# Work items of 32 rows instead of 64 in the routed-expert stage of a decoder step

## The reference, cut to what matters

```python
def swiglu(x, wg, wu, wd):
    return (jax.nn.silu(x @ wg) * (x @ wu)) @ wd
# routed: out[row] += weight * swiglu(h2[row], w_gate[e], w_up[e], w_down[e])   for the row's 8 experts e
# w_gate, w_up: 1024 x 256, w_down: 256 x 1024, all float32, 3.15 MB for each expert
```

## Time and profile before

| | us |
|---|---|
| median of 3 runs | 1567.07 |
| lowest, highest | 1562.95, 1567.58 |
| the profiled execution | 1568.95 |
| its span, first to last instruction | 1567.2 |
| PE busy in the span | 1495.0 (95%) |
| DVE, ACT, POOL busy | 649.3, 357.8, 211.9 |
| mean granted clock of TensorE | 0.976 |
| moved by DMA | 437.26 MB, mean 279 GB/s |

### The profile page before, as it was taken

How to read it: one execution, slowest core, us unless ns; L and a number is a source line. 1 busy time by engine, 2 the same in 40 slices (tenths; PEclk the granted TensorE clock), 3 DMA queues, 4 the chain that set the end, 5 groups by cost and what they waited for, 6 DMA issues and landing times.

```text
span 1567.2 us, 22305 instructions
## 1 busy us (share of the span) xinstructions
PE 1495.0 (95%) x8198; PEld 815.4 (52%) x8198; DVE 649.3 (41%) x1126; ACT 357.8 (23%) x674; POOL 211.9 (14%) x257
## 2 busy tenths in 40 slices
PE   4999999999999989999999989999999999999988
PEld 4444456777688768878545533333333333333333
DVE  4899992332231576437567811111111111111136
ACT  4111133422443324332124111111111111111120
POOL 2231101111000013100000011111111211111100
PEclk9999999999999899899999999999999999999998
DMA  9798645878422567638411699999999999989696
GB/s 341 263 324 293 248 139 194 283 278 287 145 81 81 181 210 261 228 108 302 137 54 54 242 364 419 420 419 421 370 384 407 371 421 420 416 297 414 261 368 253
DMA packets 124759, 437.26 MB, mean 279 GB/s; under 512 B 17702, under 2 KB 45722, under 8 KB 89854
## 3 DMA queue, kind: packets, MB, share of 16 engines
q1 hardware_dynamic: 95728, 323.73, 54.6%
q0 software_dynamic: 23616, 101.90, 17.5%
q10 hardware_dynamic: 5344, 10.65, 1.8%
HBM read 507.52 MB, written 45.61 MB: 353 GB/s over the span
## 4 chain that ended last, share of the span: by engine, by line
PE 83%; DMA 9%; DVE 3%; ACT 2%; issue 1%; SPq 1%; ACTq 0%; POOLq 0%; DVEq 0%
PE bank L2525 19%; PE bank L2139 14%; PE bank L2050 12%; PE bank L2550 9%; PE bank L2370 4%; DMA arena<-in_w_exp_up_dram 4%; PE bank L2358 4%; PE bank L2511 3%; PE bank L2172 2%; DMA shared_rows<-arena 1%; DMA arena<-expert_rows 1%; PE bank L2597 1%; PE bank L2396 1%; PE bank L2535 1%; PE bank L2157 1%; PE bank L2297 1%
## 5 line engine op out<-in xcount | busy, mean ns | idle before, releaser
L2525 PE MATMUL bank<-arena 128*64 128x512 f32 x1536 | 345.6, 601 | 7.5 <-DMA arena<-in_w_exp_up_dram 6.4
L2139 PE MATMUL bank<-arena 128*128 128x260 f32 x1024 | 239.8, 390 | 0.0
L2525 PEld LDWEIGHTS bank<-arena 128*64 128x64 f32 x1536 | 106.6, 136 | 210.4 <-issue 205.3
L2139 PEld LDWEIGHTS bank<-arena 128*128 128x128 f32 x1024 | 193.4, 193 | 34.5 <-ACT arena L998 2.7
L2050 PE MATMUL bank<-arena 128*128 128x512 f32 (+1 forms) x448 | 190.4, 581 | 0.0
L2550 PE MATMUL bank<-arena 128*64 128x512 f32 x768 | 175.3, 598 | 0.5 <-ACT arena L1232 0.5
L1903 DVE TENSOR_TENSOR arena<-arena,bank 128x256 f32<-128x256 f32 x48 | 20.3, 423 | 362.3 <-ACT arena L1208 362.3
L2050 PEld LDWEIGHTS bank<-arena 128*128 128x128 f32 x448 | 83.8, 190 | 98.2 <-issue 90.7
L2550 PEld LDWEIGHTS bank<-arena 128*64 128x64 f32 x768 | 50.7, 136 | 89.4 <-issue 83.1
L1208 ACT ACTIVATE arena<-bank 128x256 f32<-128x256 f32 x48 | 18.5, 385 | 335.0 <-PE bank L2525 321.8
L1919 DVE COPY arena<-bank 128x512 f32<-128x512 f32 x48 | 33.3, 693 | 137.1 <-PE bank L2550 137.1
(11 more groups left out here) (469 smaller groups left out, 1567.0 us busy)
## 6 DMA issues: line engine op xcount, KB each, us to landing
arena<-in_w_exp_gate_dram SPq DMA_DIRECT2D x96, 1024.0 KB
arena<-in_w_exp_up_dram SPq DMA_DIRECT2D x96, 1024.0 KB
arena<-in_w_exp_down_dram SPq DMA_DIRECT2D x96, 1024.0 KB
arena<-in_w_ada_dram SPq DMA_DIRECT2D x24, 1024.0 KB, 7.4
arena<-in_w_merge_gate_dram SPq DMA_DIRECT2D x16, 1024.0 KB, 6.5
arena<-expert_rows SPq DMA_DIRECT2D x16, 1024.0 KB, 10.8
arena<-in_w_in_dram SPq DMA_DIRECT2D x6, 2048.0 KB, 14.3
gate_logits<-arena ACTq DMA_DIRECT2D x32, 260.0 KB, 4.9
```

Source lines behind the costliest of these rows:

```text
L2139: last = mm(o[:, 0:HALF], gate_place(q)[:, c, ms], hT[:, c, row_half[u % 2]], start=(c == 0), stop=(c == KC - 1))
L2525: ins = mm(bank[gu_bank[q]][r, :].rearrange("p (g n) -> p g n", g=2), xT[q][:, c, r], wgu[2 * q + lane][:, :, c, :], start=(c == 0), stop= ...
```

## The change

Items have 32 rows. A block still gathers 128 rows, 64 of lane 2q and 64 of lane 2q + 1, but these are now two items of each lane, and they are worked on in two half steps h = 0 to 5 within a round of three blocks. A half step has one item of 32 rows of each of two lanes. The lane pair of half step h is h % 3, so each lane's weight places are used every third half step. `gate_up` of a half step has 32 products of 256 columns with 32 stationary rows, over four column groups (two lanes, two halves of the hidden width); `down` has 8 products of 512 columns, again over four groups (two lanes, two halves of the output width). `middle_transposed` is one transpose per half step. The weights of half step g are asked for after `gate_up` of half step g - 3, the down weights after `down` of g - 3. The down weights are read as runs of 4 KB instead of 8 KB. The scatter of a block becomes two scatters of 2 KB per row. The tables have 102 columns of half steps instead of 66 of blocks and 204 cells instead of 132, and a few small VectorE operations are added to build them. The diff, cut to its core:

```diff
-SUB = 64
+SUB = 32
 LANES = 6
-MAXP = 22
+MAXP = 17
...
+            w_expert = [A[name][0].rearrange("e (p c) n -> e p (c n)", p=P) for name in ("w_exp_gate", "w_exp_up")]
+            w_expert_down = A["w_exp_down"][0].rearrange("e (c p) n -> e p c n", p=P)
+
+            def cell_expert(cell):
+                return sp.value_load(expert_p[:, bass.ds(cell, 1)], min_val=0, max_val=MISS)
 
             def gate_up_lanes(cell, b, lanes=range(2)):
                 for lane in lanes:
-                    expert_load([wgu[2 * b + lane][:, m, :, :].rearrange("p c n -> p (c n)") for m in range(2)], (0, 1), cell + lane, f"wg{b}")
+                    e = cell_expert(cell + lane)
+                    for m in range(2):
+                        dst = wgu[2 * b + lane][:, m, :, :].rearrange("p c n -> p (c n)")
+                        sp.dma_start(dst.unsqueeze(1), w_expert[m][bass.ds(e % NE, 1)].rearrange("e p n -> p e n"), cond=e < NE).then_inc(sem[f"wg{b}"], 16)
 
             def down_lanes(cell, b, lanes=range(2)):
                 for lane in lanes:
-                    expert_load([None, None, wdn[2 * b + lane].rearrange("p c n -> p (c n)")], (2,), cell + lane, f"wd{b}")
-
-            def gate_up_load(p, q):
-
-                sp.wait_ge(sem["gu_done"], p * 3 + (q - 3))
+                    e = cell_expert(cell + lane)
+                    sp.dma_start(wdn[2 * b + lane].unsqueeze(1), w_expert_down[bass.ds(e % NE, 1)].rearrange("e p c n -> p e c n"), cond=e < NE).then_inc(sem[f"wd{b}"], 16)
+
+            def gate_up_load(p, h):
+
+                sp.wait_ge(sem["gu_done"], p * 6 + (h - 2))
                 sp.sem_inc(sem["x_col"], 1)
-                gate_up_lanes(p * 6 + (2 * q - 2), block_at(p, q, -1)[1])
-
-            def down_load(p, q):
-
-                sp.wait_ge(sem["dn_done"], p * 3 + (q - 4))
+                gate_up_lanes(p * 12 + 2 * h, h % 3)
+
+            def down_load(p, h):
+
+                sp.wait_ge(sem["dn_done"], p * 6 + (h - 2))
                 sp.sem_inc(sem["x_col"], 1)
-                down_lanes(p * 6 + (2 * q - 4), block_at(p, q, -2)[1])
+                down_lanes(p * 12 + 2 * h, h % 3)
...
-            gate_up_load(1, 1)
-            gate_up_load(1, 2)
-            down_load(1, 2)
-            with sp.Fori(2, last + 1) as p:
-                for q in range(3):
-                    gate_up_load(p, q)
-                    down_load(p, q)
-            gate_up_load(last + 1, 0)
-            down_load(last + 1, 0)
-            down_load(last + 1, 1)
+            gate_up_load(0, 3)
+            gate_up_load(0, 4)
+            down_load(0, 3)
+            gate_up_load(0, 5)
+            down_load(0, 4)
+            with sp.Fori(1, last + 1) as p:
+                for h in range(6):
+                    gate_up_load(p, h)
+                    down_load(*half_at(p, h, -1))
+            down_load(last, 5)
...
-            sp.wait_ge(sem["gu_done"], last * 3 + 1)
+            sp.wait_ge(sem["gu_done"], last * 6 + 4)
...
+            half_rows = yd.rearrange("r (m d) -> (r m) d", m=2)
+
+            def block_scatter(p, q, at):
+
+                pb, qb = block_at(p, q, -5)
+                for a, evicted in enumerate(("y_a", "y_v")):
+                    pool.wait_ge(sem[evicted], pb * 3 + (qb + 1))
+                    pool.sem_inc(sem["x_col"], 1)
+                    pool.indirect_dma_start(out=half_rows, out_offset=bass.IndirectOffsetOnAxis(ap=at[:, 1 + a:2 + a], axis=0), in_=ybuf[qb][:, a * 512:(a + 1) * 512],
+                                            in_offset=None, bounds_check=2 * TOK * TOPK - 1, oob_is_err=False).then_inc(sem[f"yst{qb}"], 16)
...
+            def gate_up(p, h):
+                g, q, a, b = p * 6 + h, h // 2, h % 2, h % 3
+                pe.wait_ge(sem[f"wg{b}"], p * 128 + 64 * (h // 3 + 1))
+                if a == 0:
+                    pe.wait_ge(sem["x_ca"], p * 3 + (q + 1))
+                    pe.wait_ge(sem["x_cv"], p * 3 + (q + 1))
+                if later(p) or h >= 3:
+
+                    pe.wait_ge(sem["m_h"], g - 2)
                 for c in range(KC):
                     for lane in range(2):
+                        tokens = xT[q][:, c, 64 * lane + SUB * a:64 * lane + SUB * a + SUB]
+                        for n in range(2):
+                            r = slice(64 * lane + SUB * n, 64 * lane + SUB * n + SUB)
+                            ins = mm(bank[gu_bank[b]][r, 0:2 * P].rearrange("p (g n) -> p g n", g=2), tokens, wgu[2 * b + lane][:, :, c, n * P:(n + 1) * P], start=(c == 0), stop=(c == KC - 1))
                 ins.then_inc(sem["gu_done"], 1)
+            def middle_transposed(p, h):
+                g = p * 6 + h
+                pe.wait_ge(sem["m_h"], g + 1)
+                if later(p) or h >= 2:
+
+                    pe.wait_ge(sem["m_hTc"], g - 1)
+                tr(bank[4][:, h % 2 * P:h % 2 * P + P], hmid[h % 3], ident).then_inc(sem["m_hT"], 1)
+
+            def down(p, h):
+                g, q, a, b = p * 6 + h, h // 2, h % 2, h % 3
+                pe.wait_ge(sem["m_hTc"], g + 1)
+                pe.wait_ge(sem[f"wd{b}"], p * 64 + 32 * (h // 3 + 1))
                 if later(p) or q:
+                    pe.wait_ge(sem["y_v" if a else "y_a"], p * 3 + q)
+                for n in range(2):
+                    for lane in range(2):
+                        for m in range(2):
+                            r = slice(64 * lane + SUB * m, 64 * lane + SUB * m + SUB)
+                            ins = mm(bank[5 + a][r, :], hmT[b][:, 64 * lane + SUB * n:64 * lane + SUB * n + SUB], wdn[2 * b + lane][:, n, m * 512:(m + 1) * 512], start=(n == 0), stop=(n == 1))
                 ins.then_inc(sem["dn_done"], 1)
+            def block(p, q, front=True):
+
+                gate_up(p, 2 * q)
+                down(*half_at(p, 2 * q, -1))
+                middle_transposed(p, 2 * q)
+                gate_up(p, 2 * q + 1)
                 if front:
                     rows_transposed(*block_at(p, q, 1))
+                down(p, 2 * q)
+                middle_transposed(p, 2 * q + 1)
...
+            def block(p, q, front=True):
+                gate(p, 2 * q)
+                middle(p, 2 * q)
+                gate(p, 2 * q + 1)
                 if front:
                     rows_half(*block_at(p, q, 1))
-                if back:
-                    result_half(*block_at(p, q, -1))
-                middle(p, q)
+                result_half(p, q)
+                middle(p, 2 * q + 1)
...
+            def block(p, q, front=True):
+                middle(p, 2 * q)
+                result_half(*block_at(p, q, -1))
+                middle(p, 2 * q + 1)
                 if front:
                     rows_half(*block_at(p, q, 1))
 
             rows_half(0, 0)
+            middle(0, 0)...
-                tt_(hb[0:n], hb[0:n], row_code[0:n, t, :].unsqueeze(2).to_broadcast([n, TOPK, MAXB]), ALU.mult).then_inc(sem["r_tab_in"], 1)
+                tt_(hb[0:n], hb[0:n], row_code[0:n, t, :].unsqueeze(2).to_broadcast([n, TOPK, MAXG]), ALU.mult).then_inc(sem["r_tab_in"], 1)
```

More of the change, by code:

```diff
@@ L1224, in result_half, with middle @@
                 act.copy(ybuf[q][:, 0:512], bank[5][:, :]).then_inc(sem["y_a"], 1)
-            def middle(p, q):
-                i = p * 3 + q
-                act.wait_ge(sem["m_hT"], i + 1)
-                if later(p):
-                    act.wait_ge(sem["dn_done"], i - 2)
-                act.copy(hmT[q], bank[4][:, 0:2 * P].rearrange("p (c n) -> p c n", n=P)).then_inc(sem["m_hTc"], 1)
-            def block(p, q, front=True, back=True):
-                gate(p, q)
+            def middle(p, h):
+                g = p * 6 + h
+                act.wait_ge(sem["m_hT"], g + 1)
+                if later(p) or h >= 3:
+                    act.wait_ge(sem["dn_done"], g - 2)
+                act.copy(hmT[h % 3], bank[4][:, h % 2 * P:h % 2 * P + P]).then_inc(sem["m_hTc"], 1)
@@ L1236, in block @@
+            def block(p, q, front=True):
+                gate(p, 2 * q)
+                middle(p, 2 * q)
+                gate(p, 2 * q + 1)
                 if front:
                     rows_half(*block_at(p, q, 1))
[L1238 to L1240 removed]
+                result_half(p, q)
+                middle(p, 2 * q + 1)
             rows_half(0, 0)
[L1243 removed]
+            gate(0, 0)
+            rows_half(0, 1)
@@ L1244, in _ @@
+            middle(0, 0)
+            gate(0, 1)
             act.wait_ge(sem["sh_out1"], 48)
+            result_half(0, 0)
+            middle(0, 1)
             for i in range(1, 6):
@@ L1831, in _ @@
             step(tt_(r_val, r_val, r_new, ALU.mult))
-            ts_(r_cells, iota_s, r_col, r_val, ALU.is_equal, ALU.mult).then_inc(sem["r_tab_in"], 1)
+            for c in range(2):
+                last = ts_(r_cells[:, c, :], iota_s, r_col[:, c:c + 1], r_val[:, c:c + 1], ALU.is_equal, ALU.mult)
+            last.then_inc(sem["r_tab_in"], 1)
             step(tt_(r_st, r_end, r_nb, ALU.subtract))
@@ L1965, in rows_done @@
```

(21 more changed lines are left out.)

228 lines of the change are left out of this document (95 added, 133 removed).

## The result

| | before | after |
|---|---|---|
| median, us | 1565.09 (4 runs) | 1637.5 (4 runs, 1633.02 to 1641.93) |
| the profiled execution, its span | 1568.95, 1567.2 | 1638.91, 1637.1 |
| end of the last down | 1512.7 | 1569.56 |
| from there to the end of the span | 54.5 | 67.5 |
| moved by DMA | 437.26 MB | 443.72 MB |

The change makes the kernel slower: ratio 1.0462, 95% interval 1.0426 to 1.0498. The forecast was 1604, range 1572 to 1622; the direction was right, the size was 34 us short and outside the range. Both are above the range. The 10 us between the two are looked at in the last experiments.

The account below looks back on a forecast made before the run. Before, TensorE paced the expert stage with the DMA close behind; after, shorter look-ahead was to make TensorE wait for weights. 1568.95 + 24 (last down) + 2 (tables) + 11 (tail) = 1606, less 1.9 to the median: 1604, range 1572 to 1622.

Parts of the forecast that it names:

- A half step's gate_up: Expert stage: 64 records of 256 columns take 3.65 us, bounds 3.52 and 4.0.
- TensorE alone: Expert stage: two half steps take 12.4 us with transposes, so TensorE without weight waits would save 62 us.
- rival C: Column groups don't overlap four deep: near 1950; by the skill's 60 cycles per matmul, near 1640. Chance 0.03.
- rival D: Skipping the load for a repeated expert fails at half steps: 168 loads, kernel near 2270. Chance 0.01.
- Rival A: Look-ahead of 15 us suffices, DMA stays full, end comes with the bytes: 1550 at 420 GB/s throughout. Chance 0.12.
- rival B: Look-ahead costs half of what the queue model gives: 1586 or somewhat less, down to no change. Chance 0.12.
- tally: Load-by-load model of the expert weights' DMA queue from 940 us, at 0.41 MB/us, giving TensorE's waits and last down's end.
- the 2 us that the prediction took off for a late wait: Kernel's end: tail grows by 13 us from the later read-back, a late wait gives back 2, leaving 11.
- 33 waits, 60 to 65 us together, 35 us of DMA pause ... I take 1537: Expert stage: queue model's weight waits put the last down at 1537, between 1540 and 1534, 24 us later than now.
- the prediction's own signs of being wrong: Expert stage: PE waits under 30 us with DMA share near 1 throughout, or a gate_up over 4 us.
- The clock's price: Expert stage: a wait above 1.5 us costs 1.7 us more, as the next gate_up runs slower.
- The DMA's pace: Expert weights' queue: 0.41 MB/us puts the last down at 1540, 0.415 at 1534.

Follow-up runs that it names:

- the last experiments: Kernel after, GpSimd's work put off in three variants: 1627.54, 1623.3, 1623.97 us; then unedited reruns of the kernel after, 1627.55, and of the first variant, 1628.44.
- the second time: The kernel after, unedited, measured and profiled once more on another occasion: 1627.55 us (5 runs), ratio 1.0390 against the kernel before.

## Why the prediction was right or wrong

**What held.** A half step's gate_up: 3.66 us where 3.65 was taken; down 1.93 with its tail; TensorE alone 59.8 us earlier where 62 were forecast. The Trainium skill (TensorEngine Tiling (Array Packing), Instruction Overhead) has about 60 cycles on top of every matmul; by the prediction's estimate that would be some 80 ns a record, and the trace differs: 3.66 us for 64 records are 57 ns. The 1640 us that rival C had by that rule lie near the measured 1637.5 by chance: the time went into waits, not into longer records. q1 moves 330.0 MB, 6.3 more, as forecast, so loads are skipped over half steps (rival D falls). Rival A, the DMA staying full, falls by the windows above; rival B by the size; rival C by the 3.66. The direction and its reason, less look-ahead with more bytes, are borne out by both look-ahead runs and by the one with fewer bytes. The waits came where they were told: in the kernel after 9.53 us before 992.57 (half step 8, tally 9.3), 8.93 before 1223.17 (half step 37, tally 5.6), 5.00 before 1258.12 (half step 41, tally 7.3), and none above 2 us from 1314 to 1417 (half steps 48 to 62). The second time the three were 9.25, 9.11 and 8.67 us. The pauses of the DMA came too: in the second run a share of 0.63 from 1135 to 1145, and 0.48 from 1360 to 1380. The read-back began 9.7 us ahead of E, where 10 were forecast; the tail grew by 13.0, and the 2 us that the prediction took off for a late wait did not come off.

**What failed: "33 waits, 60 to 65 us together, 35 us of DMA pause ... I take 1537".** E came at 1569.6, and at 1560.6 the second time.

- 9 us are the slow even gate_ups of the first occasion. They had no term. In the trace of before each gate_up behind the first block takes 7.10 us unless it had to wait for weights. A gate_up over 4 us was also one of the prediction's own signs of being wrong.
- The other 24 us are in the tally, and there in its waits. It counts from half step 3 on and has half steps 0 to 2 done by 942. The second time gate_up 2 waited 12.4 us and was done at 943.8, 2 us late. From half step 3 on TensorE waited 78.9 us for gate and up weights in 28 places and 4.0 in 1 place for down weights: 83 us together instead of 60 to 65, about 20 us of the 24. The DMA share from 940 to 1540 has a mean of 0.915, 51 us of pause instead of 35.
- Seen from the run without weights the account nearly closes: 91.3 us of waits for gate and up weights (half step 2 included), 4.0 for down weights, and a gate_up busy for 331.4 us instead of 307.7, 24 us that the half clock after waits costs. That is 119 of the 124.8 us between the two E (1560.6 - 1435.8).
- The clock's price was not what was too small. The tally adds 1.7 us for every wait above 1.5. The second time there were 20 such waits before a gate_up; 12 of them (1.9 to 12.4 us long) made it 1.4 to 2.7 us longer, and 8 (1.6 to 2.8 us) nothing: 23 us in all, where 20 times 1.7 are 34. One such place in the first profile:

```profile
1191.30:1194.00 2.70, 2.68 (x28) 1.50 (x32) 0.00 (x0) 0.00 (x0) 0.00 (x0) 0.50 1.03 411
1194.00:1197.80 3.80, 3.80 (x48) 2.06 (x44) 0.00 (x0) 0.00 (x0) 0.00 (x0) 0.59 1.03 424
```

Behind the wait that ended at 1191.32 TensorE runs at a granted clock of 0.50 while the DMA is full (1.03). This is the HAM oscillation of the Trainium skill (TensorE: Matmul & The Clock Gate), DMA waits that return the engine to its half clock, and the trace agrees for these 12 of the 29 waits.

- The DMA's pace: the prediction tried 0.41 and 0.415 MB/us (E 1540 and 1534) and took 1537 between them; the lower side was not tried. 60 us windows of the second run with a share near 1 show 389 to 417 GB/s. By the prediction's own slope, 6 us for 0.005, a pace 1% lower would move E by some 5 us, an estimate.
- Why the tally has 20 us of waits too few is not settled beyond that. The same tally was 5 us short for the shorter look-ahead on the kernel before (11 against 16) and 20 on the kernel after (1614 against 1634), but within 1.4 us for the kernel before itself: it fails where the look-ahead is short, and the prediction had checked it only where look-ahead was plentiful (three waits).

**Terms too small to matter.** 4 KB runs: 6 us of DMA were taken, about 5 by the queue's pace, and none of it in the time of the kernel before. Tables: 2 us were taken; the first gate_up starts at 916.19 instead of 915.99, 0.2 later.

**The range.** Its upper end added a longer gate_up, the silu and the runs, all sizes of products and bytes. It had nothing for the tally being wrong, though the forecast rested on a sum of 33 queue waits. With the 24 us of the tally in it, 1622 would have been 1646.

## What to carry to other kernels

When places for weights are halved in time, count the look-ahead in us against the bytes that a queue must move in it. Here going from 29 to 17 us of look-ahead cost the kernel before 20 to 23 us, and going from 15 to 9 cost the kernel after 66 to 76. Engine time saved in front of such a wait is worth nothing: 60 us of TensorE were won and 108 lost again (second time). A queue model that fits three waits is checked for three waits; give its result an error of the size by which it misses a run in the regime to be forecast. And before a small gain is put down to an edit, run the unedited kernel again beside it: here 10 us came and went with the occasion. A tail whose first load stands behind an unrelated one is worth a look by itself: moving four read-backs in front of it won the kernel before 6 us, though in the kernel after no gain was seen.

## What the runs showed of the hardware that was not expected

- TensorE's weight loads can pause with nothing waited for, at full clock: after about 40 loads two groups of four come with gaps of up to 0.6 us, in the gate_up that runs beside GpSimd's gather and two scatters. It adds about 1.2 us to a gate_up of 128 short instructions, appears at the same place in 28 of 42 blocks of one occasion and at none in another of the same kernel, and was clear in two of the ten profiles of half-step kernels and faint in a third.
- A moving operand that takes every second float32 column costs 7% (3.93 us instead of 3.66, in the even gate_ups of one run).
- An issue of a weight load on SyncE, mostly 0.33 to 0.4 us, took 5.25 at 982.41 (kernel after, second time). The loads issued from 963.38 on, for half step 8, had not all landed then (its gate_up waited until 990.84), and five more stood behind them. The DMA share was 1.02 from 982 to 991, so the queue lost nothing by it:

```profile
963.38 0.35 SPq L629 DMA_DIRECT2D arena<-in_w_exp_gate_dram  x1
...
982.41 5.25 SPq L629 DMA_DIRECT2D arena<-in_w_exp_gate_dram  x1
```
